# Second attention of a three-block network: work by residues mod 4, unscaled probabilities, and reciprocals applied at the output

## The reference, cut to what matters

```python
q = (h @ w_q).reshape(B, S, N_DIL, N_KV, GQA_R, HEAD_DIM)
for gi, (window, dilation) in enumerate(DILATIONS):
    o, lse = dilated_group_attention(q[:, :, gi], k_shared[:, :, gi], v_shared[:, :, gi], dilation, window, rel_bias)
    ...
alpha = jax.nn.softmax(jnp.stack(lses, axis=-1), axis=-1)
o = jnp.einsum("bsgrdi,bsgri->bsgrd", jnp.stack(outs, axis=-1), alpha)
```

## Time and profile before

| | |
|---|---|
| median of 3 runs | 3058.39 us (3057.18 to 3060.39) |
| span of the profiled execution | 3053.9 us |
| what lies around the span, against the median | 4.5 us |
| busy: TensorE, VectorE, ScalarE, GpSimd | 92%, 63%, 29%, 39% |
| chain that ended last, by engine | PE 45%, DMA 21%, issue 14%, DVE 8%, POOL 8%, ACT 3% |

### The profile page before, as it was taken

The page is one execution under the profiler, slowest core; times in us unless marked ns, Lnnn a source line. Parts: engine busy times, 40 slices in busy tenths (PEclk is TensorE's granted clock), DMA queues, the critical chain, the costliest instruction groups (busy, mean ns, idle before and its releaser), DMA issues.

```text
span 3053.9 us, 34662 instructions
## 1 busy us (share of the span) xinstructions
PE 2798.6 (92%) x11710; PEld 1771.9 (58%) x11710; DVE 1928.1 (63%) x5020; ACT 888.7 (29%) x1684; POOL 1189.5 (39%) x838
## 2 busy tenths in 40 slices
PE   9898999977778877799999999999999999999998
PEld 3345444432223322244448777888888877788887
DVE  8956777788888887777765985444032177554411
ACT  4732111111111111121113884222132167522222
POOL 5302333444434433343330334444444433344443
PEclk9999999999999999899999999999999999999999
DMA  3128999999999998999996112223223222122232
GB/s 126 54 89 346 420 420 413 403 421 421 421 421 421 421 422 359 407 420 419 414 414 204 50 53 83 96 96 102 95 86 100 82 84 81 43 96 96 96 104 75
DMA packets 128930, 715.86 MB, mean 234 GB/s; under 512 B 15815, under 2 KB 20583, under 8 KB 62952
## 3 DMA queue, kind: packets, MB, share of 16 engines
q0 software_dynamic: 74352, 543.04, 43.1%
q1 hardware_dynamic: 53368, 168.63, 16.3%
q10 hardware_dynamic: 1072, 2.47, 0.2%
HBM read 711.74 MB, written 2.34 MB: 234 GB/s over the span
## 4 chain that ended last, share of the span: by engine, by line
PE 45%; DMA 21%; issue 14%; DVE 8%; POOL 8%; ACT 3%; another core or an unknown queue 0%; POOLq 0%; SPq 0%; DVEq 0%; ACTq 0%
DMA arena<-in_peer_uv,arena 16%; PE ps L530 15%; PE ps L764 12%; POOL w_lo L408 6%; DMA ring<-in_peer_uv,arena 3%; PE ps L1893 3%; PE ps L1331 2%; PE ps L1345 2%; DVE arena L1048 2%; PE ps L1317 2%; PE ps L795 2%; PE ps L1954 2%; POOL arena L1110 2%; DMA n<-in_peer_uv,arena 1%; PE ps L711 1%
## 5 line engine op out<-in xcount | busy, mean ns | idle before, releaser
L764 PE MATMUL ps<-arena 128*128 128x512 f32 x1792 | 842.0, 615 | 145.9 <-DVE arena L1059 142.4
L1110 POOL DMA_INDIRECT arena<-in_peer_uv,arena x448 | 473.2, 1056 | 796.7 <-PE ps L764 647.1
L764 PEld LDWEIGHTS ps<-arena 128*128 128x128 f32 x1792 | 336.9, 195 | 602.4 <-issue 351.5
L1048 DVE CUSTOM_DVE_ANT_0 arena<-arena,sq 128x1024 f32<-128x1024 f32 x448 | 531.4, 1223 | 242.4 <-DMA arena<-in_peer_uv,arena 237.6
L408 POOL TENSOR_TENSOR w_lo<-ring,w_hi 128x1024 fp32r<-128x1024 f32 (+1 forms) x156 | 416.7, 2671 | 511.4 <-ACT w_hi L421 511.4
L530 PE MATMUL ps<-n_hi,w_hi 128*128 128x512 f32 x992 | 388.4, 392 | 0.7 <-issue 0.4
L530 PE MATMUL ps<-n_hi,w_lo 128*128 128x512 f32 x992 | 388.1, 391 | 0.0
L530 PE MATMUL ps<-n_lo,w_hi 128*128 128x512 f32 x992 | 385.7, 393 | 0.2 <-DVE n_lo L457 0.2
L912 ACT ACTIVATE arena<-arena,tok_scale 128x2 f32<-128x2 f32 x256 | 75.7, 296 | 1051.1 <-DVE arena L1048 1051.1
L421 ACT CAST w_hi<-ring 128x1024 fp32r<-128x1024 f32 (+1 forms) x156 | 173.8, 1114 | 652.0 <-PE ps L530 652.0
L530 PEld LDWEIGHTS ps<-n_hi,w_hi 128*128 128x128 f32 x992 | 186.2, 188 | 44.8 <-issue 2.6
(11 more groups left out here) (314 smaller groups left out, 4096.4 us busy)
## 6 DMA issues: line engine op xcount, KB each, us to landing
ring<-in_a_up SPq DMA_DIRECT2D x44, 512.0 KB
ring<-in_b_up SPq DMA_DIRECT2D x44, 512.0 KB
ring<-in_a_in SPq DMA_DIRECT2D x40, 512.0 KB
ring<-in_w_q SPq DMA_DIRECT2D x32, 512.0 KB
ring<-in_b_q SPq DMA_DIRECT2D x24, 512.0 KB
ring<-in_a_down SPq DMA_DIRECT2D x16, 704.0 KB
ring<-in_b_down SPq DMA_DIRECT2D x16, 704.0 KB
ring<-in_w_in SPq DMA_DIRECT2D x16, 512.0 KB
```

The lines of the kernel that those rows point to most:

```text
L764: mm = pe.matmul(bank(2 * (tt % 2) + q), diag[:, no % DIAGS, r, :], uvrow[p][r][:, D + 512 * q:D + 512 * q + 512], start=slot + r == 0, st ...
L1048: ins = dve.tensor_tensor_reduce(out=u, in0=u, in1=ntok[:, tt, :], scale=1.0, scalar=0.0, op0=ALU.mult, op1=ALU.add, accum_out=dots[:, p, ...
L1110: pool.indirect_dma_start(uvrow[p][r], None, t["peer_uv"], bass.IndirectOffsetOnAxis(ap=expert_id[:, tt, slot + r:slot + r + 1], axis=0)). ...
```

## The change

- Keys and values of branches 1 and 2 are stored by residue mod 4 (`drain_kv`), and so are the queries, which are ordered within a tile for branch 0 (`drain_near_queries`) and over all 512 tokens for branches 1 and 2 (`drain_far_queries`). A tile of 128 queries is four runs of 32 (`RUN`), one for each residue, and a run of branches 1 and 2 meets only the 32, 64, 96 or 128 keys of its own residue.
- Scores: per step 2 matmuls for branch 0 and 16 for branches 1 and 2, each with 64 rows and 32 stationary columns, which write 32 partitions. One increment follows the last. Two score banks per head alternate.
- A row holds `near + 2 * far` scores: 192, 384, 448 or 512. VectorE biases branch 0 in one instruction per head and branches 1 and 2 in another; in the last tile of a pair (but the first pair) one instruction takes all 512.
- The probabilities are not scaled. Near and far transposes have one PSUM bank each, and ScalarE copies each with one instruction. The far probabilities of four tiles are gathered in `ptFar` (cleared once) and multiplied with the values once per pair (`far_values`).
- The reciprocals of the row sums are broadcast over 64 stationary columns and multiplied with the identity into a PSUM bank of their own; VectorE copies that bank out and multiplies the output by it as it drains. GpSimd has no part in the attention any more.
- Tables: 12 transfers per pair instead of 3, in four buffers instead of two. The bias rows are shorter, so six chunks make them instead of eight.
- The first attention is computed as before; its functions are only renamed and freed of the branches for the second.

```diff
 ROWS = {
-    "sel": (511, 639, lambda d: d >= 0),
-    "win": (383, 511, lambda d: (d >= 0) & (d <= 255)),
-    "dil0": (255, 383, lambda d: (d >= 0) & (d <= 128)),
-    "dil1": (511, 639, lambda d: (d >= 0) & (d % 4 == 0)),
-    "dil2": (511, 639, lambda d: (d >= 0) & (d % 16 == 0)),
+    "sel": (511, 639, 1, lambda d: d >= 0),
+    "win": (383, 511, 1, lambda d: (d >= 0) & (d <= 255)),
+    "dil0": (255, 383, 1, lambda d: (d >= 0) & (d <= 128)),
+    "dil1": (P - 1, P - 1 + RUN, RES, lambda d: d >= 0),
+    "dil2": (P - 1, P - 1 + RUN, RES, lambda d: (d >= 0) & (d % 16 == 0)),
 }
...
-ptB = b.take(2, 20 * P)
-pB = Pieces([b.take(2 * 1280), b.take(2 * 1280), kvB.rearrange("p a b -> p (a b)")[:, 6 * T:6 * T + 2 * 1280]])
...
+ptFar = b.take(2, 4 * RES, TT * RUN)
...
+ptNear = b.take(2, 4 * P)
+pB = b.take(3, 2, 4 * P)
...
+TABS = 4
+tabB = n[:, :, :].rearrange("p a b -> p (a b)").rearrange("p (x y d) -> p x y d", x=TABS, y=2)
+first_near = std[:, :].rearrange("p (y d) -> p y d", y=2)
+first_far = ring[:, 0:2, D:D + 2 * P]
...
-BIAS_AT = [LATE_GROUPS + x for x in (4, 5, 6, 7, 10, 11, 12, 13)]
+BIAS_AT = [LATE_GROUPS + x for x in (4, 5, 6, 7, 10, 11)]
...
-            pr = L.p[:, s % 3, 0:sum(b.width for b in sides[0].values())]
-            ins = dve.tensor_scalar(pr, pr, L.inv[:, s % 3, 0:1], None, ALU.mult)
-            b, by = sides[1][2], L.inv[:, s % 3, 1:2]
-            pr = L.p[:, s % 3, 1280:1280 + side[0].width + side[1].width]
-            ins = pool.tensor_scalar(pr, pr, L.inv[:, s % 3, 1:2], None, ALU.mult)
...
+def by_residue(ap):
+    return ap.rearrange("p (k r) -> p r k", r=RES)[:, ::-1, ::-1]
+def near_columns(ap, qt):
+    return ap.rearrange("p (r a k) -> p r a k", r=RES, a=TT)[:, :, TT - 1 - qt, :]
+def spans(s):
+    it, qt = divmod(s, TT)
+    return it, qt, it // GR, min(2, qt + 1) * P, RUN * (qt + 1)
...
+NEAR_BANK, FAR_BANK, INV_BANK = 4, 5, 7
+def dilated_pe(pe):
+    def scores(s):
+        it, qt, gp, near, far = spans(s)
+        if s >= 2:
+            pe.wait_ge(LB.bank_read, reads_before(s - 1))
+        rows = [slice(64 * half, 64 * half + 64) for half in range(2)]
+        for half in range(2):
+            pe.matmul(ps[:, score_bank(s, half), 2 * P - near:2 * P], qB[rows[half], it, P * qt:P * qt + P],
+                      kvB[rows[half], gp, P * (qt + 1) - near:P * (qt + 1)], start=True, stop=True)
+        for d in (1, 2):
+            for r in range(RES):
+                at, q, keys = P * (d + 2) - far, P * r + RUN * (TT - 1 - qt), P * (RES - 1 - r)
+                for half in range(2):
+                    mm = pe.matmul(ps[RUN * r:RUN * r + RUN, score_bank(s, half), at:at + far],
+                                   qB[rows[half], 8 * d + it, q:q + RUN], kvB[rows[half], 2 * d + gp, keys:keys + far],
+                                   start=True, stop=True)
+        mm.then_inc(LB.scores_ready, 1)
+    def turn(s):
+        it, qt, gp, near, far = spans(s)
+        if s:
+            pe.wait_ge(LB.near_copied, s)
+        for half in range(2):
+            pe.wait_ge(LB.exp_done, 2 * s + half + 1)
+            for x in range(near // P):
+                at = near * half + P * x
+                tr = pe.transpose(ps[:, NEAR_BANK, at:at + P], pB[:, s % 3, half, P * x:P * x + P], ident)
+            if half:
+                tr.then_inc(LB.turned, 1)
+            elif s:
+                pe.wait_ge(LB.far_copied, s)
+            for d in range(2):
+                at = P * (2 * half + d)
+                tr = pe.transpose(ps[0:far, FAR_BANK, at:at + P], pB[:, s % 3, half, near + far * d:near + far * (d + 1)],
+                                  ident)
+        tr.then_inc(LB.turned, 1)
+    def near_values(s):
+        it, qt, gp, near, far = spans(s)
+        pe.wait_ge(LB.near_copied, s + 1)
+        if qt == 0 and it:
+            pe.wait_ge(LB.o_drained, it)
+        for x in range(near // P):
+            for half in range(2):
+                lo = 64 * half
+                kv, at = 64 * (2 * gp + half), near * half + P * x
+                mm = pe.matmul(near_columns(bank(OUT_BANK)[lo:lo + 64], qt), vtokB[:, 0, qt + 1 - near // P + x, kv:kv + 64], ptNear[:, s % 2, at:at + P],
+                               start=qt == 0, stop=False)
+        pe.wait_ge(LB.inv_ready, s + 1)
+        for half in range(2):
+            lo = 64 * half
+            mm = pe.matmul(near_columns(bank(INV_BANK)[lo:lo + 64], qt),
+                           invB[:, s % 3, half:half + 1].broadcast_to([P, 64]), ident, start=qt == 0,
+                           stop=qt == TT - 1)
+        mm.then_inc(LB.near_done, 1)
+    def far_values(it):
+        gp = it // GR
+        pe.wait_ge(LB.far_copied, TT * (it + 1))
+        for d in (1, 2):
+            for r in range(RES):
+                for half in range(2):
+                    kv = 64 * (2 * gp + half)
+                    mm = pe.matmul(ps[64 * half:64 * half + 64, OUT_BANK, P * r:P * r + P],
+                                   vtokB[:, d, RES - 1 - r, kv:kv + 64], ptFar[:, it % 2, RES * (2 * half + d - 1) + r, :],
+                                   start=False, stop=d == 2 and r == RES - 1)
+        mm.then_inc(LB.pv_done, 1)
+    scores(0)
+    for s in range(STEPS + 2):
+        if s + 1 < STEPS:
+            scores(s + 1)
+        if s >= 2:
+            near_values(s - 2)
+            if (s - 2) % TT == TT - 1:
+                far_values((s - 2) // TT)
+        if 1 <= s <= STEPS:
+            turn(s - 1)
+def dilated_dve(dve):
+    def row_max(s):
+        it, qt, gp, near, far = spans(s)
+        if qt == 0:
+            if it:
+                dve.wait_ge(LB.tab_in[it % TABS], 16 * LOADS * (1 + (it > TABS)))
+            else:
+                dve.wait_ge(first_tabs_in, 16 * LOADS)
...
+        dve.wait_ge(LB.scores_ready, s + 1)
+        near_tab = tabB[:, it % TABS, :, 0:2 * P] if it else first_near
+        far_tab = tabB[:, it % TABS, :, 2 * P:4 * P] if it else first_far
+        def biased(to, src, tab, half, slot):
+            dve.tensor_tensor_reduce(out=to, in0=src, in1=tab, scale=1.0, scalar=-FLOOR, op0=ALU.add, op1=ALU.min,
+                                     accum_out=mxB[:, s % 3, half, slot:slot + 1]).then_inc(LB.bank_read, 1)
+        for half in range(2):
+            pr, src = pB[:, s % 3, half, :], bank(score_bank(s, half))
+            if joined(s):
+                biased(pr, src, tabB[:, it % TABS, half, :], half, 2)
+                continue
+            biased(pr[:, 0:near], src[:, 2 * P - near:2 * P], near_tab[:, half, 2 * P - near:2 * P], half, 0)
+            to = pr[:, near:near + 2 * far].rearrange("p (d c) -> p d c", d=2)
+            parts = (x.rearrange("p (d c) -> p d c", d=2)[:, :, P - far:P] for x in (src[:, 2 * P:4 * P], far_tab[:, half, :]))
+            biased(to, *parts, half, 1)
+        if not joined(s):
+            dve.wait_ge(LB.bank_read, reads_before(s + 1))
+            dve.tensor_reduce(mxB[:, s % 3, :, 2:3], mxB[:, s % 3, :, 0:2], AX_X, ALU.min).then_inc(LB.max_ready, 1)
+    def inverse(s):
+        if s >= 3:
+            dve.wait_ge(LB.near_done, s - 2)
+        dve.wait_ge(LB.exp_done, 2 * s + 2)
+        dve.reciprocal(invB[:, s % 3], denB[:, s % 3]).then_inc(LB.inv_ready, 1)
+    def drain(it):
+        dve.wait_ge(LB.pv_done, it + 1)
+        out, inv = (bank(x).rearrange("p (r k) -> p k r", r=RES)[:, ::-1, ::-1] for x in (OUT_BANK, INV_BANK))
+        to = attn[:, it, :].rearrange("p (k r) -> p k r", r=RES)
+        dve.tensor_copy(to, inv).then_inc(LB.inv_kept, 1)
+        dve.wait_ge(LB.inv_kept, it + 1)
+        dve.tensor_tensor(to, out, to, ALU.mult).then_inc(LB.o_drained, 1)
+    for s in range(STEPS + 2):
+        if s < STEPS:
+            row_max(s)
+        if 1 <= s <= STEPS:
+            inverse(s - 1)
+        if s >= 2 and (s - 2) % TT == TT - 1:
+            drain((s - 2) // TT)
+def dilated_act(act):
...
+    def copies(s):
+        it, qt, gp, near, far = spans(s)
+        act.wait_ge(LB.turned, 2 * s + 1)
+        if s >= 2:
+            act.wait_ge(LB.near_done, s - 1)
+        act.copy(ptNear[:, s % 2, 0:2 * near], bank(NEAR_BANK)[:, 0:2 * near]).then_inc(LB.near_copied, 1)
+        act.wait_ge(LB.turned, 2 * s + 2)
+        if qt == 0 and it >= 2:
+            act.wait_ge(LB.pv_done, it - 1)
+        act.copy(ptFar[0:far, it % 2, :, RUN * (TT - 1 - qt):RUN * (TT - qt)],
+                 bank(FAR_BANK)[0:far].rearrange("p (x k) -> p x k", k=RUN)).then_inc(LB.far_copied, 1)
+    act.wait_ge(LB.far_cleared, 1)
+    for s in range(STEPS + 1):
+        if s < STEPS:
+            exponentials(s)
+        if s:
+            copies(s - 1)
+    act.wait_ge(LB.pv_done, 8)
...
+LOADS = 3 * RES
+def load_tables(sp, it, near, far, landed):
+    for r in range(RES):
+        rows = slice(RUN * r, RUN * r + RUN)
+        sp.dma_start(near[rows], near_rows(heads(it)[0], r)).then_inc(landed, 16)
+        for d in (1, 2):
```

(54 more changed lines are left out.)

373 lines of the change are left out of this document (163 added, 210 removed).

## The result

| | before | after |
|---|---|---|
| time, median (lowest to highest) | 3058.76 us (4 runs) | 2987.51 us (2981.09 to 2991.95, 4 runs) |
| ratio after / before | | 0.9765 [0.975, 0.9779] |
| second attention, from the end of the last query drain to the output projection | 182.1 us | 110.7 us |
| one pair of heads | 21.99 us | 13.35 us |

The kernel became 71.3 us faster; 44.6 us were forecast. Rival 1 (all eight tiles side by side) had given 2994. The profiled execution of the changed kernel took 2991.95 us, with a span of 2990.2, so 1.8 us lie around the span. The 4.5 us given for the kernel before were the distance of one execution's span from the median of others; the forecast used them before and after alike, so its difference of 44.6 does not depend on them.

A forecast was written before the change was run, and what follows sets the result against it. TensorE was taken to set each pair of heads: 8 x 16.5 + 5.5 = 137.5 us for the stage against 182.1, so span 3009.3, plus 4.5 gives 3013.8 us. The range was 2988 to 3044.

The forecast's parts named there:

- Rival 1: Far scores, second attention: all eight tiles run side by side, about 13 ns a record, pair 14.0, time 2994 us; chance 0.25.
- the price of a far-score record: Far scores, second attention: 33 ns for each of 128 records a pair, two tiles overlapping, 4.2 us.
- near scores: Branch 0 scores on TensorE, second attention: 2.5 us per pair of heads.
- transposes: TensorE, second attention: 30 transposes a pair instead of 54, 4.0 us, so 3.0 less.
- near values: TensorE, second attention: near value matmuls with those spreading the reciprocals, 44 records, 3.0 us a pair.
- far values: TensorE, second attention: run once per pair, 16 matmuls, 32 records, 1.8 us.
- waits: TensorE waiting for copies or VectorE's drain within a pair: no time added, taken as covered by its other work.
- fill and empty: Start and end of the second attention, outside the eight pairs: 6.2 us becomes about 5.5, bounds 4.5 and 8.
- Rivals 2 and 3: Far scores: feeding limit or serial, 55 to 69 ns, 3036 to 3051 us, 0.22; full-width cost, 109 ns, 3092, 0.06 with clock fall.
- the cover: TensorE's turn and scores hide VectorE's 1.4 us drain before a pair's first near values; failing costs up to 1.5 a pair.
- an x under 13 ns: Sign of a wrong forecast: price of a far-score record in the second attention beyond 13 or 55 ns.
- the bounds: Very last query drain, the only exposed one: between -0.1 and +0.7 us if strided reads were twice as slow.

The follow-up runs named there:

- second set apart: Changed kernel with all far score matmuls of a step issued twice, the second round after the whole first one; 2993.41 us, stage 119.3 us.
- the first experiment: Changed kernel with far score matmuls issued twice, the heads ordered 0, 1, 0, 1 within each branch and residue; 3001.49 us, stage 124.6 us.

## Why the prediction was wrong

**The failed step** is the price of a far-score record: "Nearest: ... I take 33 ns ... More tiles in parallel would need instructions to be fed faster than any row shows." It measured 8 ns without the changes of kind ((1.75 - 4 x 0.17) / 128), at the lower bound of 9 that stood beside it (6 ns with the forecast's own 0.24 for a change of kind). With the changes of kind the term is 1.75 us instead of 5.2: 3.4 us a pair and 27 us in the stage, which was off by 26.8. The other errors nearly cancel (-1.4 us near scores, -1.0 transposes, -0.8 near values, +0.4 far values, +5.2 waits, -1.6 fill and empty).

The reading that failed is that of the earlier trace rows. The 31 ns a record there were taken as near the rate at which TensorE can be fed. They were the rate of two tiles, each busy with its own records. One rule, worked out from the groups of this case, gives those of the table within 0.08 us: **0.17 us, and the number of records on one tile times the longer of the tile's weight load and its stream** (stationary columns / 1.2 ns; twice the moving columns / 2.4 ns). The 0.17 is fitted to the four far groups after, and what takes this time was not shown. The rates are those of the groups on two tiles: 107 ns a record with 128 columns, moving or stationary.

| group | tiles | records a tile, ns each | rule, us | measured |
|---|---|---|---|---|
| far scores, 64 / 96 / 128 columns | 8 | 4 x 53 / 80 / 107 | 0.38 / 0.49 / 0.60 | 0.38 / 0.49 / 0.60 |
| far scores, 32 columns | 8 | 4 x 27 | 0.28 | 0.28 |
| near scores, 256 columns | 2 | 2 x 213 | 0.60 | 0.63 |
| far values | 2 | 16 x 107 | 1.88 | 1.85 |
| 64 stationary, 32 / 128 columns | 4 | 8 x 53 / 107 | 0.60 / 1.02 | 0.62 / 1.09 |
| 128 stationary, 32 / 128 columns | 2 | 16 x 107 | 1.88 | 1.80 / 1.88 |
| second set apart, 128 columns | 8 | 8 x 107 | 1.02 | 1.08 |
|, 62 columns | 2 | 4 x 53 | 0.38 | 0.39 |
|, 31 stationary | 1 | 16 x 53 | 1.02 | 1.01 |

The last two rows are of before. The rule could have been read there for one and two tiles; that it holds for eight is what rival 1 supposed, and would have given 0.60 us for 128 columns. The rule has exceptions. Twelve score records of before with 128 columns took 1.10 us against 0.81, and an order with neighbours on the same tiles costs more (1.37 us against 1.02 in the first experiment). Short streams leave it above 32 records: 64 records of 32 columns took 0.68 us with the second set apart, against 0.38, and the 48 of near and far scores 0.71 against 0.49. The second 32 records thus cost 0.40 us, 12.5 ns each. A limit of feeding is a possible cause; it would lie far under the 33 ns of the forecast, and the far groups of the changed kernel follow the rule without it.

**Rival 1** is what happened, even below its 13 ns. Its stage of 117.5 us is 8 x 14.0 + 5.5, with no term for the waits that it names. Measured were 8 x 13.35 + 3.9, the 0.65 us of waiting included. The page that it named (the Trainium skill, TensorEngine Tiling (Array Packing), section Key Properties: different tiles load and multiply in parallel) agrees with the runs up to eight tiles. The rule from its section Instruction Overhead, some 60 cycles for every short matmul (25 ns by estimate), does not hold across tiles: 16 matmuls of 32 columns, 32 records, took 0.28 us, 18 ns a matmul and 9 ns a record, and the measurement decides. **Rivals 2 and 3** (55 to 109 ns) fell with the four far groups, and the clock of the changed kernel's stage did not fall.

**The other steps.** Transposes, values, reciprocal matmuls and near scores came within 0.2 us a pair of their terms: prices per record and group carried over as long as the form had a row. VectorE under 10 us held (7.2 busy), and ScalarE was busy for 8.7 us where 11 were forecast; the exponential of 512 columns was measured at 719 ns for a forecast of 715. The waits were put at nothing with up to 1.5 us if the cover fails: it failed by 0.65, by the route through the drain and with ScalarE's near copy at its end. So the chain does not run almost only through TensorE, as forecast; that was one of the forecast's own signs of being wrong, beside an x under 13 ns. Fill and empty took 3.9 us (110.7 - 8 x 13.35) for 5.5.

**Outside the stage.** The last query drain shows the strided reading, 0.38 us over the 0.69 of the earlier trace rows and inside the bounds. The first eight tiles' drains were put at 1.1 us and as covered; the last of them stands in the chain with 1.26. The last query drain stands in the chain shown above; this is the other one, in the chain of the same kernel:

```profile
2340.74 1.26 DVE arena L1761 x4
```

That is some 0.6 us more than one drain of before, so about 1 us in all against nothing. SyncE's 12 first tables take 5.5 us of issue (2296.89 to 2302.4) for the 5.6 forecast. The median moved by 71.3 us and the stage by 71.4; whether the missing 1 us is there can't be told under the 12 us by which the stage's start moves (in the two profiled executions it starts 7.6 us later after than before, 2456.5 and 2448.9).

## What to carry to other kernels

Before pricing a small matmul from a row, count how many tiles of the array that row used, and divide its time by the records that one tile had to do; only a group with many tiles, short streams and many records shows what TensorE can be fed. Spread small matmuls over all tiles, with neighbours in the order on different tiles. A chain of waits that leaves the bounding engine for 5 us is worth only the time for which that engine stands still. Read it from the starts of its groups, with and without the wait. Before pricing a part of a change from one stage time, compare the steady pairs and look at the granted clock of the first.

## What was not expected of the hardware

- Eight tiles of 64 rows and 32 columns side by side take a record every 9 ns (32 in 0.28 us), and every 19 ns with streams of 128 columns (0.60). With 64 records of 32 columns, the second 32 cost 12.5 ns each.
- Doubling the stationary columns at the same streams took the 128-column group from 0.60 to 1.09 and 1.88 us.
- The order of 64 records over the tiles is worth 0.29 us (1.08 or 1.37); with 32 records it is worth 0.05.
- A drain of 512 columns that reads every fourth column takes 1.07 us, one that reads them in order 0.69.
- Taking 42 us of VectorE's and 68 of GpSimd's work out of a stage that TensorE bounds changed it by 0.1 us.
- At the start of the stage the granted clock fell to 1.2 GHz in two of the runs, for some 3.5 and 6.4 us. TensorE had stood idle for 1.28 us in front of the stage in the first, and for 1.29 and 1.91 us in the second. The changed kernel had 1.28 and 0.92 us there and kept 1.00 in both of its traces.
